# Even mixer: columns in order of need, gates along the tokens with one scan, u's products between the heads, attention's rows of the output first

## The reference

```
h = rms_norm(x, norm_mix[0])
u_a, v_a, q, k, v_b, f = jnp.split(h @ ev_w_in, splits, axis=-1)   # 512 each, f has 8
y_a = gelu(u_a) * (tril(w_s) @ rms_norm(gelu(v_a), v_gain) + b_s)  # 4 groups, 128 tokens
c   = cumsum(log_sigmoid(f + b_f), axis=1)                         # 8 heads, along tokens
s   = rms_norm(q) @ rms_norm(k).T / 8 + c[query] - c[key]          # causal, 8 heads of 64
y_b = softmax(s) @ v_b
x   = x + concat([y_a, y_b]) @ ev_w_out
```

## Time and profile before

| | us |
|---|---|
| median of 3 runs | 4089.4 (4087.97 to 4091.43) |
| the profiled execution: its own time | 4091.04 |
| its span | 4089.2 |
| PE busy in it | 3557.0 (87%) |
| mean granted TensorE clock | 0.962 of 2.4 GHz |
| the stage, from PE's first turn (3190.0) to its last product (3349.3) | 159.3 |

### The profile page before, as it was taken

One profiled execution on the slowest core, in us unless ns is written; L12 is line 12 of the kernel. 1 busy time (PEld: TensorE's weight loads), 2 busy tenths in 40 slices (PEclk: granted clock), 3 DMA queues, 4 the chain that ended last, 5 costly groups with the idle time before them and its releaser, 6 DMA issues.

```text
span 4089.2 us, 57374 instructions
## 1 busy us (share of the span) xinstructions
PE 3557.0 (87%) x21617; PEld 1945.4 (48%) x21617; DVE 2474.7 (61%) x5806; ACT 1085.3 (27%) x2893; POOL 1261.1 (31%) x1294
## 2 busy tenths in 40 slices
PE   7988999889899977778988988887777889999999
PEld 3567444764544432223333445442322468655774
DVE  3556445653666677777688755677775348545441
ACT  2354114531322222232223542222222121010100
POOL 1154004430234444444444412344443010025000
PEclk9988999889999999999999999999999989999999
DMA  8311264102899999999999957999999334421443
GB/s 290 118 44 35 103 202 148 37 24 83 313 404 408 417 419 422 413 416 414 413 395 422 421 206 289 415 419 420 418 418 408 97 93 138 149 88 42 143 148 123
DMA packets 282699, 1060.71 MB, mean 259 GB/s; under 512 B 24139, under 2 KB 108502, under 8 KB 184122
## 3 DMA queue, kind: packets, MB, share of 16 engines
q0 software_dynamic: 115248, 815.69, 48.8%
q1 hardware_dynamic: 167178, 241.34, 17.9%
HBM read 1055.49 MB, written 1.46 MB: 258 GB/s over the span
## 4 chain that ended last, share of the span: by engine, by line
PE 54%; DMA 26%; DVE 10%; ACT 4%; issue 3%; POOL 3%; DVEq 0%; POOLq 0%; ACTq 0%
DMA arena<-in_peer_uv,arena 25%; PE psum L2022 12%; PE psum L266 11%; PE psum L304 7%; PE psum L853 5%; PE psum L1980 4%; DVE arena L2171 3%; PE psum L905 3%; PE psum L218 2%; PE psum L1252 1%; PE psum L1396 1%; POOL arena L3644 1%; PE psum L1304 1%; POOL arena L3643 1%; PE psum L1315 1%
## 5 line engine op out<-in xcount | busy, mean ns | idle before, releaser
L2022 PE MATMUL psum<-arena 128*128 128x512 f32 x3072 | 1460.8, 618 | 329.5 <-ACT arena L2060 327.2
L2171 DVE SCALAR_TENSOR_TENSOR arena<-arena 128x1024 bf16<-128x1024 f32 x768 | 940.8, 1225 | 488.5 <-DMA arena<-in_peer_uv,arena 464.6
L2121 POOL DMA_INDIRECT arena<-in_peer_uv,arena x768 | 868.8, 1131 | 1168.9 <-PE psum L2022 1041.6
L2022 PEld LDWEIGHTS psum<-arena 128*128 128x128 f32 x3072 | 572.3, 195 | 1129.5 <-issue 564.7
L266 PE MATMUL psum<-ring,arena 128*128 128x512 f32 (+1 forms) x1088 | 464.9, 588 | 14.4 <-DVE arena L3457 4.4
L2053 ACT ACTIVATE arena<-arena 128x2 f32<-128x2 f32 x384 | 78.2, 204 | 1176.8 <-DVE arena L2171 1176.4
L266 PEld LDWEIGHTS psum<-ring,arena 128*128 128x128 f32 x1088 | 206.0, 193 | 268.9 <-issue 251.3
L2060 ACT ACTIVATE arena<-consts,arena 128x128 f32<-128x128 f32 x768 | 270.6, 394 | 224.8 <-DVE arena L2183 222.6
L304 PE MATMUL psum<-arena,ring 128*128 128x256 f32 x1408 | 305.3, 379 | 1.8 <-ACT arena L352 1.8
L304 PEld LDWEIGHTS psum<-arena,ring 128*128 128x128 f32 x1408 | 267.0, 190 | 38.0 <-ACT arena L352 2.0
L853 PE MATMUL psum<-arena,ring 128*128 128x512 f32 x512 | 234.0, 604 | 1.6 <-issue 1.6
(11 more groups left out here) (501 smaller groups left out, 4040.1 us busy)
## 6 DMA issues: line engine op xcount, KB each, us to landing
arena<-in_ada_w SPq DMA_DIRECT2D x48, 1024.0 KB, 7.1
ring<-in_ffn_w_up SPq DMA_DIRECT2D x44, 1024.0 KB, 5.1
ring<-in_dn_w_in SPq DMA_DIRECT2D x24, 1024.0 KB, 6.7
ring<-in_peer_w_query SPq DMA_DIRECT2D x22, 1024.0 KB, 11.2
ring<-in_ffn_w_down SPq DMA_DIRECT2D x20, 1024.0 KB, 5.0
arena<-in_peer_uv,arena POOLq DMA_INDIRECT x768, 12.7
ring<-in_ev_w_in SPq DMA_DIRECT2D x10, 1024.0 KB, 5.0
arena<-gc_d SPq DMA_DIRECT2D x32, 256.0 KB, 3.0
```

What stands on the lines that cost most here:

```text
L2022: m = e.matmul(k.banks[4 + t % 2 * 2 + nh], self.diag[g % self.ND], self.vsl[g % self.NS][:, nh * 512:(nh + 1) * 512], start=u % 8 == 0 an ...
L2121: e.indirect_dma_start(self.uv[g % self.NS], None, self.table(), bass.IndirectOffsetOnAxis(ap=self.eid[u % 6][:, s:s + 1], axis=0)).then_i ...
L2171: e.scalar_tensor_tensor(self.junk[g % 2], self.us[g % self.NS], 1.0, self.h[:, u // 8, :], MUL, MUL, accum_out=self.a[u % 2][:, s:s + 1]) ...
```

## The change

The stage is written anew, with the same arithmetic but for the way in which the running sum is made. On PE:

- The groups come in the order q, k, v_a, v_b, u (`pe_cols`). The 8 columns f are no group any more: POOL loads them at the stage's start (`wf`), and 8 products with the weights' 8 columns as the stationary side give f as 8 rows by 256 tokens, behind q.
- The turns of the spatial weights stand behind f, those of q behind k's group, those of k behind v_a's.
- log-sigmoid is done on 8 x 256 by DVE and ACT while k's group runs, and one scan of DVE along the tokens makes the running sum; two turns bring it into the other layout.
- `pe_heads` takes one product of u's group (a generator; `next(u)`) behind the scores of each head.
- The attention's half of y is turned first, the products of v_a follow, then the blocks of `ev_w_out` go in the order (columns 0, rows 512 up), (columns 512, rows 512 up), and the same two with rows 0 to 511; y_a's half is turned behind the first block.

On the other engines ACT makes the squares of q, k and v_a straight out of PSUM or SBUF, DVE scales q and k straight out of PSUM (no copies), 1/8 goes into q's gain once, and ACT copies v_b out. gelu of u moves behind the heads. The values of the heads use two PSUM banks in turn, not four.

The core of the diff:

```
 class EvenMixer(Stage):
+
+
+    Q, KK, VA, VB, U = 1024, 1536, 512, 2048, 0
...
-        self.dst = [self.u, self.va, self.q, self.kk, self.vb]
-        self.proj = TokenProj(self, "in", self.hT, 8, W, 2568, 2, lambda t, n0: (S if n0 < 1024 else V).at(("z", t, n0)))
...
-        self.at = Attend(self, lambda n: self.Ss[n % 2][:, 0:128 * (n // 8 + 1)], lambda n: 128 * (n // 8 + 1),
...
     def sp(self, e):
-        self.proj.sp(e)
-        self.out.sp(e)
+        k = self.k
+        for n0 in (self.Q, self.KK, self.VA, self.VB, self.U):
...
+                load_block(k, e, self.key("in", n0, k0), self.W, k0, 4, n0, 512)
+        for n0, k0 in self.out_blocks():
+            load_block(k, e, self.key("out", n0, k0), k.i["ev_w_out_2"][0], k0, 4, n0, 512)
...
+    def out_blocks(self):
+        return ((0, 4), (512, 4), (0, 0), (512, 0))
...
-        for dst, src in ((self.vg, "ev_v_norm_2"), (self.qg, "ev_q_norm_2"), (self.kg, "ev_k_norm_2"), (self.fb, "ev_b_fgate_2")):
+        e.dma_start(self.wf, self.W[:, 2560:2568].rearrange("(k p) n -> p k n", p=128)).then_inc(*self.lf.up())
+        e.dma_start(self.fb[0:8, :], k.i["ev_b_fgate_2"][0].rearrange("(h o) -> h o", o=1)).then_inc(*self.lf.up("f"))
...
+    def pe_cols(self, e, n0, free=None):
...
+                    e.wait_ge(*free(t))
+                for q in range(4):
+                    m = e.matmul(self.proj_bank(n0, t), self.hT[:, k0 + q, t * 128:(t + 1) * 128], w[:, q, :], start=k0 + q == 0,
+                                 stop=k0 + q == 7)
+                    if q < 3:
+                        yield
...
+                yield
...
+    def pe_turn(self, e, g):
+        src, dst, t = self.turned[g]
+        e.wait_ge(*self.V.at(("unit", self.Q if g < 2 else self.KK, t)))
+        for c in range(4):
+            m = self.turn(e, self.k.banks[g][:, c * 128:(c + 1) * 128], src[:, t, c * 128:(c + 1) * 128])
+        m.then_inc(*self.P.up(("t", g)))
...
-        self.proj.pe(e)
-        e.wait_ge(*V.at(("z", 1, 2560)))
-        self.qkt.pe(e)
+        for _ in self.pe_cols(e, self.Q):
+            pass
+        e.wait_ge(*self.lf.at("f"))
+        for q in range(8):
+            m = e.matmul(k.banks[3][0:8, 0:256], self.wf[:, q, :], self.hT[:, q, :], start=q == 0, stop=q == 7)
+        m.then_inc(*P.up("f"))
...
         for g in range(4):
-            m = self.turn(e, k.banks[0][:, g * 128:(g + 1) * 128], self.ws[:, g, :])
+            m = self.turn(e, k.banks[2][:, g * 128:(g + 1) * 128], self.ws[:, g, :])
         m.then_inc(*P.up("ws"))
+        for _ in self.pe_cols(e, self.KK):
+            pass
+        for g in (0, 1):
+            self.pe_turn(e, g)
+        for _ in self.pe_cols(e, self.VA, lambda t: V.at(("scaled", self.Q, t))):
+            pass
         e.wait_ge(*V.at("ws"))
+        e.wait_ge(*V.at("f"))
+        for g in (2, 3):
+            self.pe_turn(e, g)
...
+        e.wait_ge(*V.at("cz"))
...
-            e.wait_ge(*(V.at(("qkT", "T", 2)) if t else S.at(("qkT", "T", 1))))
+            m = self.turn(e, k.banks[0][:, t * 8:t * 8 + 8], self.cz[0:8, t * 128:(t + 1) * 128])
+        m.then_inc(*P.up("c8"))
+        for _ in self.pe_cols(e, self.VB, lambda t: V.at(("scaled", self.KK, t))):
+            pass
+        e.wait_ge(*G.at("qz"))
+        e.wait_ge(*self.ls.at("s"))
+        e.wait_ge(*V.at("c8"))
+        e.wait_ge(*V.at(("T", 2)))
+        e.wait_ge(*S.at(("T", 3)))
+        self.pe_heads(e, self.pe_cols(e, self.U, lambda t: S.at(("va", t))))
...
+        for t in range(2):
+            e.wait_ge(*V.at(("put", 8 * t + 7)))
+            for c in range(4):
+                m = self.turn(e, k.banks[t][:, c * 128:(c + 1) * 128], self.y[:, t, 512 + c * 128:640 + c * 128])
+            m.then_inc(*P.up(("yt", t, 1)))
...
-        b = k.banks[3]
...
-        e.wait_ge(*S.at(("qkT", "T", 3)))
-        e.matmul(b[:, 0:8], k.const("le"), self.lf[:, 0, :], start=True, stop=True)
-        e.matmul(b[:, 8:16], k.const("ones"), self.lf[:, 0, :], start=True, stop=False)
-        e.matmul(b[:, 8:16], k.const("le"), self.lf[:, 1, :], start=False, stop=True).then_inc(*P.up("c8"))
-        e.wait_ge(*V.at("c8"))
+        for n0, k0 in self.out_blocks():
...
+            for t in range(2):
+                e.wait_ge(*(S if t else V).at(("yT", t, k0 // 4)))
+                for q in range(4):
+                    m = e.matmul(self.out_bank(t, n0), self.yT[:, k0 + q, t * 128:(t + 1) * 128], w[:, q, :], start=q == 0 and k0 == 4,
+                                 stop=q == 3 and k0 == 0)
+                m.then_inc(*P.up(("out", t, n0) if k0 == 0 else None))
...
+            if (n0, k0) == (0, 4):
+                for t in range(2):
+                    e.wait_ge(*V.at(("y", t)))
+                    for c in range(4):
+                        m = self.turn(e, k.banks[6 + t][:, c * 128:(c + 1) * 128], self.y[:, t, c * 128:(c + 1) * 128])
+                    m.then_inc(*P.up(("yt", t, 0)))
...
+    def pe_heads(self, e, u):
...
+                e.matmul(b[:, 0:nk], self.sel[:, h, :], self.cz[:, 0:nk], start=False, stop=True).then_inc(*P.up(("s", n)))
+                next(u)
...
+                    e.wait_ge(*V.at(("put", n - 2)))
...
-        self.at.pe(e, scores)
-        self.yt.pe(e)
-        for mark in self.yt.marks():
-            e.wait_ge(*mark)
-        self.out.pe(e)
...
+            e.activation(self.sq[t], src(t), ACT.Square, bias=0.0, scale=1.0).then_inc(*self.S.up(("sq", n0, t)))
...
+        self.act_squares(e, self.Q, lambda t: self.proj_bank(self.Q, t))
+        self.act_roots(e, self.Q)
+        sp = self.sp_[0:8, :]
+        e.wait_ge(*V.at("f"))
...
+        k.root_table(e)
+        self.act_squares(e, self.KK, lambda t: self.proj_bank(self.KK, t))
+        self.act_turned(e, 1)
+        self.act_roots(e, self.KK)
+        for t in range(2):
+            e.wait_ge(*P.at(("z", t, self.VA)))
+            e.activation(self.va[:, t, :], self.proj_bank(self.VA, t), ACT.Gelu_apprx_tanh, bias=0.0, scale=1.0).then_inc(*S.up(("va", t)))
+        self.act_squares(e, self.VA, lambda t: self.va[:, t, :])
+        self.act_turned(e, 3)
+        self.act_roots(e, self.VA)
...
+        for t in range(2):
+            e.wait_ge(*P.at(("z", t, self.U)))
+            e.activation(self.u[:, t, :], self.proj_bank(self.U, t), ACT.Gelu_apprx_tanh, bias=0.0, scale=1.0).then_inc(*S.up(("u", t)))
+        self.act_out(e, 1)
+        self.act_out(e, 0)
...
+    def dve_units(self, e, n0, heads, src, dst, gain):
...
+            e.reciprocal(st, st).then_inc(*V.up())
+            e.wait_ge(*V.now())
+            e.tensor_tensor(y, x, st.unsqueeze(2).to_broadcast([128, heads, 512 // heads]), MUL).then_inc(*V.up(("scaled", n0, t)))
+            e.wait_ge(*V.now())
+            e.tensor_tensor(y, y, gain, MUL).then_inc(*V.up(("unit", n0, t)))
...
+        e.tensor_scalar(self.qg, self.qg, 0.125, None, MUL).then_inc(*V.up())
+        self.dve_means(e, self.Q, 8)
+        self.dve_units(e, self.Q, 8, lambda t: self.proj_bank(self.Q, t), self.q, wide(self.qg))
...
+        e.tensor_scalar(self.lx[0:8, :], k.banks[3][0:8, 0:256], self.fb[0:8, :], -1.0, ADD, MUL).then_inc(*V.up("f"))
...
+        e.tensor_tensor_scan(self.cz[0:8, :], self.one[0:8, :], sp, 0.0, MUL, ADD).then_inc(*V.up("cz"))
+        self.dve_means(e, self.KK, 8)
+        self.dve_turned(e, 0)
+        self.dve_units(e, self.KK, 8, lambda t: self.proj_bank(self.KK, t), self.kk, wide(self.kg))
...
+        self.dve_out(e, 1)
         for t in range(2):
+            e.wait_ge(*S.at(("u", t)))
```

More of the change, by code:

```diff
@@ L2976, in __init__ @@
+        self.mx, self.sm = k.al(16), k.al(16)
         self.yT = k.al2(8, 256)
[L2977 to L2980, removed]
+        self.turned = [(self.q, self.qT, 0), (self.q, self.qT, 1), (self.kk, self.kT, 0), (self.kk, self.kT, 1)]
@@ L2993, in pool @@
         e.dma_start(self.causal, k.i["consts"][:, co:co + 512].rearrange("p (a b) -> p a b", a=2)).then_inc(*self.lt.up("t"))
+        e.memset(self.one, 1.0).then_inc(*G.up())
+        e.memset(self.cz, 0.0).then_inc(*G.up("zero"))
         for n in range(2):
[L2995 to L2998, removed]
+            e.memset(self.qz[n], 0.0).then_inc(*G.up())
@@ new lines, in proj_bank @@
+    def proj_bank(self, n0, t):
+        return self.k.banks[(4 if n0 in (self.KK, self.VB) else 6) + t]
+    def pe_cols(self, e, n0, free=None):
+        k, P = self.k, self.P
+        for k0 in (0, 4):
+            key = self.key("in", n0, k0)
+            e.wait_ge(*k.ring.ready(key))
+            w = k.ring.buf(key).rearrange("p (k n) -> p k n", k=4)
+            for t in range(2):
+                if k0 == 0 and free is not None:
+                    e.wait_ge(*free(t))
[4 more added lines that the diff above has]
+                        yield
+                if k0 or t:
+                    m.then_inc(*P.up(("z", t, n0) if k0 else None))
+                if t:
+                    k.ring.free(key, P)
+                yield
```

(38 more changed lines are left out.)

255 lines of the change are left out of this document (145 added, 110 removed).

## The result

The changed kernel takes **4067.95 us** (median of 7 runs, 4062.49 to 4079.58), the kernel before, run beside it, 4091.43 (7 runs, 4087.97 to 4098.99). The ratio is 0.9942, with an interval of 0.9929 to 0.9954: faster by 0.5 to 0.7%. The profiled execution took 4067.95 too, its span is 4066.1 us, its mean clock 0.968.

A forecast was written before the change was run, and what follows sets the result against it. In the stage, PE was taken to bound the groups and output, and the order of work the stretch between. Terms summed to 130.59 us against 151.05, gain 20.5; 4089.4 - 20.5 = 4068.9 us, range 4065 to 4076.5.

The forecast's parts named there:

- What bounds the kernel: In the stage, PE bounds groups and output; between them the order of work does, leaving nothing to fill the chain's waits.
- Groups, f, turns and hand-overs: Work ahead of the heads, with all hand-overs: 54.92 for four groups, 3.51 for f, 2.60 for turns, 0.50 for hand-overs.
- The rule weighed: Skill's rule that transposes do not engage full clock: 36 turns would cost 3.8 us more, gain 16.7; forecast kept 20.5.
- Covers: Chains on DVE, ACT and loads costed at nothing, since PE has other work until their results are wanted.
- the two places named as tightest: First head's exponential, about 2.7 us behind the group, and ACT's 2.5 us of gelu work behind the last head.
- Heads: Sixteen heads with u's 13.73 inside and 0.2 for the last: 37.13 us; ends 36 and 42.93.
- rival 5: Better: no hand-over costs, waits inside steps vanish, weight loads hide under u; 3 to 4 us more, 4065.5; chance 8%.
- Behind the heads: From last head to last output product: turns 0.94 and 0.94, wait 0.3, v_a's products 2.05, output 27.70 us.
- Narrow work at half clock (1): The 36 turns and v_a's products run at 1.2 GHz: gain 14.6, time 4074.8; chance 15%.
- heads at half clock (3): Heads with u run at 1.2 GHz: 36.9 us more, time 4105.8, slower; chance 4%.
- u in the way (2): u's product lengthens each head's chain: heads and u 42.9 instead of 37.1, gain 14.7, time 4074.7; chance 8%.
- Nothing came back to the old time (4): Rival of no change: the gain comes back in a stage behind, something there being fixed in time; 4089, chance 3%.

The follow-up runs named there:

- k last: Changed kernel with the column groups in the order q, v_b, v_a, k, u, so k's comes last ahead of the heads: stage 133.95 us, whole time 4076.66.
- late gates: Changed kernel with the gates' eight products, log-sigmoid and scan right ahead of the heads, behind v_b's group, not q's: stage 133.98 us, whole time 4079.75.
- the early gain: Changed kernel with the final norm's gain loaded on SP's queue during the stage before: whole time 4070.32 us, ratio 0.9942 to the kernel before.

## Why the prediction was right, and where it was off

- *What bounds the kernel.* Right. Order was the bound: u ahead of the heads, with all else of the change in place, gives 151.05 - 133.07 = 18.0 us, and u between the heads the other 7.3. That the order counts is shown by k last and by late gates, 8.2 us each. In the 18.0 lie also the cheaper f, the turns at full clock and the shorter chain of the gates; what the scan, or the work moved between DVE and ACT, is worth by itself, no run shows.
- *Groups, f, turns and hand-overs.* 61.31 us for 54.92 + 3.51 + 2.60 + 0.50 = 61.53: nearly all of the 0.5 for hand-overs was not needed. The weights with 8 columns cost f nothing extra (3.62 for 3.51), and the turns ran at 1.00.
- *The rule weighed.* The Trainium skill ("TensorE: Matmul & The Clock Gate", Part 4, PE-mode transpose) says that the full clock does not engage for transposes. All batches of turns in this stage ran at a clock of 1.00: 8 turns took 1.04 us, where half clock had 16 in 3.57. So the 3.8 us that the rule would have cost did not come, as the forecast had it from the earlier trace rows. These turns stand between dense products, so the runs don't show what turns alone can hold.
- *Covers.* All held. From the first product at 3199.03 the scan ended at 24.1 us (forecast 24.5), k's norm at 37.2 (37), v_a's at 53.3 (54), and the first exponential 2.4 behind v_b's group (2.7):

```profile
3222.46 0.68 DVE L3285 TENSOR_TENSOR_SCAN arena<-arena 8x256 f32<-8x256 f32 x1
...
3235.55 0.69 DVE L3251 TENSOR_TENSOR arena<-arena 128x512 f32<-128x512 f32 x1
...
3251.68 0.69 DVE L3251 TENSOR_TENSOR arena<-arena 128x512 f32<-128x512 f32 x1
```

```profile
3261.16 1.28 ACT L3217 ACT_TABLE_LOAD   x1
3262.46 0.40 ACT L3217 ACTIVATE arena<-arena 128x128 f32<-128x128 f32 x1
```

  (DVE, then ACT, in order of time.) Of the two places named as tightest the first exponential was one, as the run with u behind the turn shows; behind the last head there was 0.38 of wait ahead of it and none after. f's weights landed in 2.8 us, between the two ends given.
- *Heads.* **The mis-sized term**: "8 x 1.08 + 8 x 1.82 = 23.20. With u's 13.73 that is 36.93", 37.13 with the last head; measured 33.13. It held two errors of opposite sign, +3.28 - 7.28 = -4.00:
  - The bare heads were read too short; at full clock they take 26.68, not 23.4. 1.08 is the quick one of a pair of 1.50 and 1.08 (1.7 us over eight heads), 1.82 the quick one of 1.88 and 1.82 (0.2), and the ends of the first and last heads were nearly left out (1.4).
  - u's product was added whole, 13.73, as if a step had no room, while the filled heads cost only 6.45 more than bare ones.

  So the 5.8 us that the text had for the heads were all for the clock (29.20 to 23.4) and none for the filling. By the runs some 2.5 are for the clock (29.20 at 0.85, bare heads 26.68 at 1.00; an estimate, as the two kernels differ in more) and 7.3 for the filling. That the waits inside a step would vanish was the text's rival 5, with a chance of 8%, and its lower end, 36. By the stage it is what came, 4.8 us beyond the forecast; both were too timid, since they took the waits out of 23.2.
- *Behind the heads.* 31.34 for 31.93.
- *Rivals.* Narrow work at half clock (1) and heads at half clock (3) did not come: clock 1.00 in all three stretches. But 3's mechanism is real where PE has waited, as the runs with k last and with late gates show (0.53 and 0.54 for some 5 us). u in the way (2) is the reverse of what happened. Nothing came back to the old time (4): the next stage's first turns moved by 24.49 us (3350.12 to 3325.63).
- *The time.* The stage gave 25.3, not 20.5, and the median of the runs 23.5 (4091.43 - 4067.95). A too small gain, taken from a median (4089.4) that later runs put 2 us higher, came out 1 us from the result. The stage at 125.78 lies below the text's own bounds, 127 to 137, by the heads' 4.0. The mechanism, chains covered by independent products, was right, and its price in the heads was not; that the figure came so close was luck.

## What to carry to other kernels

Price a step by the mean of several, not by one distance in the trace: the steps here went in pairs, and the quick one is half the story. A product put into a step that waits on other engines costs its time less the wait, so take the step's own work on the bound engine and add to that. The quick bare step with 256 keys, which has no wait, gives 1.69 + 0.86 = 2.55 us as an upper end; measured were 2.39, since beside u the own work was 1.53. A second product in a step cost its whole 0.86 here (with 128 keys; with 256 it was not tried). Put first what starts the longest chain to the next meeting of engines: the same instructions in another order cost 8 us twice here, 2 of them after the wait had ended, by the clock.

## What the runs showed that was not expected

- The 24 idle turns, the same instructions in every kernel that has them, took 4.30 to 5.38 us: the clock rises at another moment within them (0.62 on average over them in the profile after, 0.51 in the one with the early gain). This moves the first group by up to 1.2 us.
- Behind the norm's 16 turns at 0.52 and 0.50 the first group ran at once at full clock in one execution and at 0.57 for 5 us in the other (13.97 and 16.10 us). One profile does not settle what such turns are worth.
- Some 6.5 us in which PE does little ahead of the heads are followed by 5 us near half clock, twice alike: 4.95 and 4.88 us for the start of the heads, with k last and with late gates, and 30.41 for the rest of them in both.
